# A streaming encoder step: key projections as one chunk of split products beside the first glu chunk

## The reference, cut

```python
h = rmsnorm(x, g_norm_mix[l]) * (1 + scale_m) + shift_m      # mod = silu(c) @ w_ada[l] + b_ada[l], six parts
q, k, v, iq, ik, iw, glu, sc, gates = split(h @ w_in[l])     # k, v, ik: 64 columns each
# A: indexer scores from iq, ik, iw choose keys; softmax attention over the chosen ones
# B: u = a * sigmoid(g); 31-tap depthwise convolution, layernorm, silu
# C: gated convolution of 3 taps
merged = g_a * (attn @ w_branch[0]) + g_b * (conf @ w_branch[1]) + g_c * (short @ w_branch[2])
x = x + gate_m * (merged @ w_out[l])
h = rmsnorm(x, g_norm_ffn[l]) * (1 + scale_f) + shift_f
x = x + gate_f * (swiglu(h) if l % 2 == 0 else top2_of_8_experts(h))
# outputs: final rmsnorm of x, new k, v, ik rows and the last convolution inputs of each layer
```

## Time and profile before

| | us |
|---|---|
| median of 3 runs | 1413.51 (1412.73 to 1415.42) |
| profiled execution | 1415.98 |
| its span | 1414.2 |
| PE busy | 1367.7 (97%) |
| DVE busy | 1012.7 (72%) |
| ACT busy | 783.3 (55%) |

### The profile page before, as it was taken

The page is one execution under the profiler, slowest core; times in us unless marked ns, Lnnn a source line. Parts: engine busy times, 40 slices in busy tenths (PEclk is TensorE's granted clock), DMA queues, the critical chain, the costliest instruction groups (busy, mean ns, idle before and its releaser), DMA issues.

```text
span 1414.2 us, 25016 instructions
## 1 busy us (share of the span) xinstructions
PE 1367.7 (97%) x9589; PEld 1211.1 (86%) x9589; DVE 1012.7 (72%) x1404; ACT 783.3 (55%) x1076; POOL 44.1 (3%) x66
## 2 busy tenths in 40 slices
PE   5999999999999999999999999998999999999997
PEld 4889999877899999997999998777588888888885
DVE  1477999875554444245789998755798988898887
ACT  1534447734453333235544486344778887788764
POOL 0010100000000000000001000000200000000030
PEclk9899999999999999999999999999999999999999
DMA  9957744224646867636578762245999999999993
GB/s 324 239 167 227 248 134 138 63 88 157 207 132 198 256 198 231 217 120 186 153 229 273 213 188 90 75 161 180 264 354 383 383 382 384 377 386 386 374 380 142
DMA packets 282693, 328.43 MB, mean 232 GB/s; under 512 B 34654, under 2 KB 192806, under 8 KB 282598
## 3 DMA queue, kind: packets, MB, share of 16 engines
q1 hardware_dynamic: 276146, 317.18, 68.4%
q0 software_dynamic: 1472, 5.24, 1.4%
q10 hardware_dynamic: 4980, 4.69, 1.0%
HBM read 312.41 MB, written 14.66 MB: 231 GB/s over the span
## 4 chain that ended last, share of the span: by engine, by line
PE 88%; DVE 6%; ACT 2%; issue 1%; DMA 1%; ACTq 0%; DVEq 0%; SPq 0%
PE mmp L915 15%; PE mmp L917 14%; PE mmp L916 14%; PE mmp L1413 8%; PE mmp L1414 8%; PE mmp L1415 8%; PE mmp L909 6%; DVE conv L2152 2%; PE px L980 1%; PE lg L980 1%; PE px L1181 1%; DMA ring<-in_w_ada_dram 1%; DMA wide<-in_w_dw_conf_dram 1%; PE lg L1137 1%; PE lg L1162 1%
## 5 line engine op out<-in xcount | busy, mean ns | idle before, releaser
L915 PE MATMUL mmp<-hT_hi,wm_hi 128*128 128x320 f32 (+1 forms) x976 | 311.3, 319 | 3.3 <-issue 3.1
L917 PE MATMUL mmp<-hT_hi,ring_lo 128*128 128x320 f32 (+1 forms) x976 | 303.0, 310 | 0.0
L916 PE MATMUL mmp<-hT_lo,wm_hi 128*128 128x320 f32 (+1 forms) x848 | 262.2, 309 | 0.0
L2063 DVE TENSOR_TENSOR ring_lo<-ring,wm_hi 128x1024 fp32r<-128x1024 f32 (+1 forms) x124 | 148.3, 1201 | 66.8 <-ACT wm_hi L1627 64.3
L915 PEld LDWEIGHTS mmp<-hT_hi,wm_hi 128*128 128x128 f32 (+1 forms) x976 | 183.6, 188 | 7.7 <-issue 5.5
L917 PEld LDWEIGHTS mmp<-hT_hi,ring_lo 128*128 128x128 f32 (+1 forms) x976 | 183.9, 188 | 0.2
L1627 ACT CAST wm_hi<-ring 128x1024 fp32r<-128x1024 f32 (+1 forms) x124 | 126.8, 1031 | 80.8 <-PE mmp L917 76.6
L916 PEld LDWEIGHTS mmp<-hT_lo,wm_hi 128*128 128x128 f32 (+1 forms) x848 | 160.0, 189 | 0.2
L1584 ACT ACTIVATE tmp<-mmp 128x320 f32<-128x320 f32 x68 | 29.8, 438 | 201.8 <-PE mmp L917 150.7
L2295 DVE TENSOR_TENSOR more_lo<-more,we_hi_a 128x2048 fp32r<-128x2048 f32 (+2 forms) x64 | 128.1, 2021 | 16.3 <-ACT we_hi_a L1811 16.2
L2152 DVE SCALAR_TENSOR_TENSOR conv<-u_conf,dwc,conv 128x350 f32<-128x350 f32 x240 | 132.6, 583 | 3.1
(11 more groups left out here) (408 smaller groups left out, 2848.6 us busy)
## 6 DMA issues: line engine op xcount, KB each, us to landing
ring<-in_w_in_dram SPq DMA_DIRECT2D x104, 512.0 KB, 4.9
ring<-in_w_exp_in_dram SPq DMA_DIRECT2D x64, 512.0 KB, 7.9
more<-in_w_exp_in_dram SPq DMA_DIRECT2D x64, 512.0 KB, 11.3
ring<-in_w_ada_dram SPq DMA_DIRECT2D x52, 512.0 KB, 6.9
more<-in_w_exp_out_dram SPq DMA_DIRECT2D x48, 512.0 KB, 6.4
wide<-in_w_ada_dram SPq DMA_DIRECT2D x44, 512.0 KB, 7.3
ring<-in_w_ffn_in_dram SPq DMA_DIRECT2D x44, 512.0 KB, 5.3
ring<-in_w_branch_dram SPq DMA_DIRECT2D x48, 256.0 KB, 2.9
```

Source lines behind the costliest of these rows:

```text
L915: nc.tensor.matmul(out, w_hi, x_hi, start=is_first, stop=False)
L916: nc.tensor.matmul(out, w_hi, x_lo, start=False, stop=False)
L917: return nc.tensor.matmul(out, w_lo, x_hi, start=False, stop=is_last)
L2063: V.tensor_tensor(mix_rows(ring_lo, l, s, r), mix_rows(ring, l, s, r), mix_hi(l, s, r).bitcast(F32), ALU.subtract).then_inc(mix_lo_ready, 1)
```

## The change

K and index-K become one split chunk `kik` of 64 + 64 columns, loaded once, the new chunk 0 of `SPLIT`; all the tables move up by one. Chunk 0 and glu 0 are worked together in a new PE function `first_chunks`: for each block f of h the three key products, and three blocks behind (`LEAD = 3`) the six glu products. DVE makes `hT_lo` two blocks behind the norm multiplication, ACT casts each block right after its scale. In layer 0 the casts and subtractions of the glu 0 weights are put between those blocks; in layer 1 those of both chunks are moved to the end of the layer-0 feed-forward, on DVE ahead of the last additions to x. The copies of the keys to both partition halves are made by ACT from PSUM (four large copies, then four small ones). In layer 0 the fifth modulation pair (m = 4) goes behind chunk 6 (glu 2), each later one takes the place of its follower, and pair 9 goes behind chunk 17, with its bank freed by the state copies. In layer 1 pair 7 stands behind `first_chunks`, and its turn one chunk later.

```diff
-ADA_AT_QKV = ((4,), (6, 7))
-ADA_AT_SPLIT = ({5: 5, 7: 6, 9: 7, 11: 8, 13: 9}, {7: 8, 9: 9, 11: 10, 13: 11})
+ADA_AT_QKV = ((), (6, 7))
+ADA_AT_SPLIT = ({6: 4, 8: 5, 10: 6, 12: 7, 14: 8, 17: 9}, {8: 8, 10: 9, 12: 10, 14: 11})
-SPLIT = ([("glu", 0), ("glu", 1), ("qkv", 2), ...
+SPLIT = ([("kik", 0), ("glu", 0), ("glu", 1), ("qkv", 2), ...
+LEAD = 3
...
# SP
+                    if s == 2:
+                        for m in ADA_AT_QKV[l][1:]:
+                            sp.wait_ge(chunk_done, ring_no["ffn", l - 1, NFFN - 1] + 1)
+                            ada_loads(l, m)
+                    if stage == "kik":
+                        v = slot_view(n % SLOTS, DC, P)
+                        load(n, [(v[:, :, r * HD:(r + 1) * HD], win[:, :, c:c + HD]) for r, c in enumerate((K0, IK0))])
...
# PE
+            def first_chunks(l):
...
+                def step(s, f):
+                    r, i = f // 4, f % 4
+                    q = pair_no[(SPLIT[s][0], l, SPLIT[s][1])]
+                    if f == 0:
+                        pair_wait(q)
+                    if i == 0:
+                        pe.wait_ge(mix_lo_ready, 2 * (NSPLIT * l + s) + r + 1)
+                    hi, lo = rows(s, r)
+                    for b in range(s + 1):
+                        c = slice(b * P, b * P + P)
+                        ins = three(mmp[:, 2 * (q % 2) + b, 0:T], hi[:, i, c], lo[:, i, c], hT_hi[:, f, :],
+                                    hT_lo[:, f, :], f == 0, f == DC - 1)
+                    if i == 3:
+                        ins.then_inc((half_done, chunk_done)[r], 1)
+
+                for f in range(DC + LEAD):
+                    if f < DC:
+                        pe.wait_ge(hT_lo_ready, DC * l + f + 1)
+                        step(0, f)
+                    if f >= LEAD:
+                        step(1, f - LEAD)
...
# ada_wait
+                    if m == ADA_AT_SPLIT[0][S_STATE + 1]:
+                        pe.wait_ge(st_copied, 3)
...
# ACT
+                    for r in range(2):
+                        mix_high(0, r)
...
                 for c in range(DC):
+                    norm_scale(2 * l, gain_of(0), shift_of(0), (c,))
                     act.wait_ge(h_ready, DC * 2 * l + c + 1)
                     copy(hT_hi[:, c, :], hT[:, c, :]).then_inc(hT_hi_ready, 1)
+                    if l == 0 and c in (1, 3):
+                        mix_high(1, c // 2)
                 if l == 0:
                     row_loads(1)
...
+                    if stage == "kik":
+                        for r, dst in enumerate((kT, ikT)):
+                            src = pair("kik", l, 0, 0)[r * HD:(r + 1) * HD, :]
+                            copy(dst[0:HD, 0:T], src)
+                            ins = copy(dst[HD:P, 0:T], src)
+                        ins.then_inc(pair_evac, 1)
+                        act.wait_ge(pair_evac, pair_no["kik", l, 0] + 1)
+                        for dst, dst_s in ((kT, kTs), (ikT, ikTs)):
+                            copy(dst[:, T:TW], dst[:, TP:T])
+                            ins = copy(dst_s[:, l, PAST:NKS], dst[:, TP:T])
+                        ins.then_inc(keys_copied, 1)
+                        return
...
# ACT, behind the loop of the layer-0 feed-forward
+                    for s in range(2):
+                        for r in range(2):
+                            mix_high(s, r, l + 1)
...
# DVE
+                norm_apply(2 * l, behind=hT_low, lag=2,
+                           beside={2: key_lows, 4: lambda: mix_low(1, 0), 6: lambda: mix_low(1, 1)} if l == 0 else ())
...
# DVE, in the loop of the layer-0 feed-forward
+                        if k == NFFN - 2:
+                            for s in range(2):
+                                for r in range(2):
+                                    mix_low(s, r, l + 1)
```

More of the change, by code:

```diff
@@ L136, in plan @@
     for l in range(DEPTH):
-        m = ADA_AT_QKV[l][0]
-        ring["ada", l, 2 * m], n = n, n + 1
-        if l:
-            ring["ada", l, 2 * m + 1], n = n, n + 1
-        for j in range(2):
-            chunk("qkv", l, j)
-        if l == 0:
-            ring["ada", l, 2 * m + 1], n = n, n + 1
+        for m in ADA_AT_QKV[l][:1]:
+            ada(l, m)
         for m in ADA_AT_QKV[l][1:]:
@@ L451, in build @@
         kv_copied = sem("kv_copied")
+        keys_copied = sem("keys_copied")
         sc_done = sem("sc_done")
@@ L705, in _ @@
                             clear_rows(j)
-                    if s == 3 and l == 0:
+                    if s == 4 and l == 0:
                         cache_loads()
@@ L1107, in _ @@
                     norm_sums(2 * l)
-                ada_half(l, ADA_AT_QKV[l][0], 0, (lambda: norm_spread(2 * l)) if l else None)
-                if l:
-                    ada_half(l, ADA_AT_QKV[l][0], 1)
-                pair_chunk("qkv", l, 0, h_rhs, blocks=((0, P),), width=P, each=h_each(2 * l))
-                pair_chunk("qkv", l, 1, h_rhs, blocks=((0, P),), width=P)
-                if l == 0:
-                    ada_half(l, ADA_AT_QKV[l][0], 1)
+                for m in ADA_AT_QKV[l][:1]:
+                    ada_half(l, m, 0, lambda: norm_spread(2 * l))
+                    ada_half(l, m, 1)
+                first_chunks(l)
                 for m in ADA_AT_QKV[l][1:]:
@@ L1218, in unit_tick @@
                         transposes(t - 1)
-                for s in range(NPROJ):
+                for s in range(2, NPROJ):
                     heads, ticks = HEADS_AT.get(s, ()), TICKS_AT.get(s, ())
@@ L1594, in shift_of, with mix_high @@
                     return lambda c: mods[:, l, 24 * which + c, 0:1]
+                def mix_high(s, r, l=l):
+                    n = ring_no[(SPLIT[s][0], l, SPLIT[s][1])]
+                    act.wait_ge(w_full[n % SLOTS], 32 * (n // SLOTS + 1))
+                    if s >= 2 and r == 0:
+                        act.wait_ge(half_done, NSPLIT * l + s - 1)
+                    if s >= 2 and r == 1:
+                        act.wait_ge(chunk_done, ring_no[(SPLIT[s - 2][0], l, SPLIT[s - 2][1])] + 1)
+                    copy(mix_hi(l, s, r), mix_rows(ring, l, s, r)).then_inc(mix_hi_ready, 1)
                 if l == 0:
@@ L1757, in _ @@
                         ada_evac(l, ADA_AT_SPLIT[l][s])
-                    if s == 0:
+                    if s == 1:
+                        for m in ADA_AT_QKV[l]:
+                            ada_evac(l, m)
+                    if s == 2:
                         for m in ADA_AT_QKV[l]:
@@ L2022, in norm_stats, with norm_apply @@
                 dve.wait_ge(rstd_spread, k + 1)
-            def norm_apply(k, behind=None, lag=0):
+            def norm_apply(k, behind=None, lag=0, beside=()):
                 for c in range(DC + 1):
+                    if c in beside:
+                        beside[c]()
                     if c < DC:
```

90 lines of the change are left out of this document (29 added, 61 removed).

## The result

The changed kernel takes 1416.72 us (median of 20 runs), the kernel before 1413.64 us beside it (20 runs): a ratio of 1.0019, 95% interval 1.0012 to 1.0026. Measured once more it took 1416.75 against 1413.89, 1.0021 (1.0012 to 1.0031). So the change makes the kernel slower, by 2.7 to 3.1 us; 1416.3 was predicted. By the count of its products it saves TensorE 5 us of work in each layer, and all of that is gone again, and a little more.

The account below looks back on a forecast made before the run. TensorE, 88% of the chain, was taken as the bound. Layer 0 (-1.0 + 1.5 + 2.0 = +2.5) and layer 1 (+3.0 - 4.0 + 1.3 = +0.3) give +2.8 on the 1413.5 median: 1416.3 us, range 1411.5 to 1419.0.

Parts of the forecast that it names:

- Layer 0, the front: Layer 0's key and glu 0 blocks: last scale ends at 49.0 us, PE through at about 55 (53 to 57).
- Layer 0, what is late next: Layer 0: loads on ACT's queue hold glu 1 until 58.5 us instead of 59.5; gain -1.0 (-0.6 to -4.5).
- glu 1 before 56: Layer 0: sign that the prediction is wrong, if glu 1 starts before 56 us; forecast start 58.5.
- The clock in layer 0: Layer 0, behind the pause ahead of glu 1: about 12 products at half clock, +1.5 us; 0 if it stays up.
- The sixth pair among the chunks: Layer 0's later chunks: six modulation pairs instead of five, with no idle PE time to hide it, +2.0 us (1.9 to 2.1).
- The wait for three copies: Layer 0: last modulation pair, behind the state transposes, waits for its bank; 0, at most one copy, 0.5 us.
- The end of the feed-forward: Before layer 1's norm: glu weights land at 640.4, subtractions delay the last addition to 647.0 us; +3.0 (+2.2 to +3.5).
- Layer 1, the keys: Layer 1's first chunks: -4.0 us, with the feed-forward's 3.0 -1.0; half clock on 11 products +1.3; layer +0.3.
- (b): One or both stretches stay at full clock: 1414.8 with layer 0, 1415.0 with layer 1, 1413.5 both; chance 0.27.
- (c): Layer 0 blocks overlap, queue drains faster, glu 1 starts before 56; with a faster layer 1, 1409.2 us; chance 0.12.
- (d): Layer 0: key weights land later than 35.4, their casts delay the first scale; +1.8, 1418.1 us, to 1420; chance 0.16.
- The base: Whole kernel: profiled execution before, 1415.98 us, lies 2.5 above the median 1413.5; same difference taken off the forecast.

Follow-up runs that it names:

- fillers: Changed kernel plus products nobody reads in PE's pauses ahead of layer 0's glu 1 and in layer 1's first block waits: 1414.22 us, ratio 1.0004.
- before_rows_sp: Kernel before, with the 13 small loads issued by SP behind its load of glu 1 instead of by ACT: 1414.20 us, ratio 1.0006.
- a_rows_on_sp: Changed kernel with the 13 small loads issued by SP behind the fourth chunk's load instead of by ACT: 1413.22 us, ratio 0.9989.
- e_pair4_cache: Changed kernel with layer 0's modulation pair 4 inside the cache transposes, five pairs left among the chunks: 1412.04 us, ratio 0.9988.
- b_tail: Changed kernel with layer 1's glu 0 casts and subtractions moved from the feed-forward's end into the norm and blocks: 1413.33 us, ratio 0.9994.
- b2_tail: Changed kernel with layer 1's glu 0 subtractions moved behind the last addition and behind the reciprocal, norm gains computed earlier: 1414.61 us, ratio 1.0007.
- c_pair4_gap: Changed kernel with layer 0's modulation pair 4 in the pause ahead of glu 1, five pairs left among the chunks: 1413.60 us, ratio 0.9995.
- best: Changed kernel with loads on SP, feed-forward's end rearranged, layer 1's pair 7 in block waits, layer 0's pair 4 in cache transposes: 1402.71 us, ratio 0.9925.

## Why the prediction held, step by step

The forecast of 1416.3 lies 0.4 us beside the 1416.72, and the mechanisms were the right ones, but that it is so close is partly luck. Glu 1 of layer 0 started 1.0 us earlier than I had put it, and the clock in layer 1 usually costs 1.3 us more; the two errors cancel.

**Layer 0, the front: right.** The last scale ended at 49.1 (49.0 predicted), the two chunks at 55.7 (55).

**Layer 0, what is late next: right in kind, 1 us too dear.** The queue of 13 loads holds glu 1, as the move to SP shows. It took 5.5 us and not 7.0, because the last entry took 0.54 us instead of the 2.06 of the earlier trace rows; glu 1 started 2.0 us earlier than before, not 1.0, and PE stood 1.80 us, not 3.5. What ends the wait is the last of the four key copies on ACT (57.41), the release of the PSUM pair, 0.36 us behind DVE's subtraction (57.05); I had the two ending together. I also misread the kernel before: the cast at 56.44 was qkv 2's, and glu 1 stood ahead of the loads. The sum doesn't suffer, as it goes from the start of glu 1, but two things exposed the wait and not one: the cover got shorter, and the list moved up by one, which put glu 1 behind the loads. My own sign of being wrong, glu 1 before 56, is a clock time and a bad sign: in the second profile glu 1 starts at 55.69, after the same pause (1.84 us), because all the blocks lie 2.0 us earlier.

**The clock in layer 0: right, with a wrong base.** 12 products at half clock, as predicted. Glu 1 to the first cache transposition takes 15.7 us with the fall and 14.1 to 14.3 without, so 1.5 us was the right size. It was there in four of the six profiles of the changed order with that pause idle, and in none with fillers, with pair 4 or without a pause. But the execution that I summed against had such a fall too, in glu 0, and before_rows_sp, the same kernel but for the 13 loads, has none behind the same pause. The fall is a draw in either kernel, so part of the +1.5 was in the base already.

**The sixth pair among the chunks: right.** +2.0 predicted, and 2.0 between the averages of the third stretch with six pairs and with five. The wait for three copies cost nothing that the timelines show.

**The end of the feed-forward: right.** Landing 640.4 predicted, 640.97 found; last addition 647.0 predicted, 647.23 found; +3.0 against the feed-forward's own end, and taking the two subtractions out brings 3.0 back.

**Layer 1, the keys: right in its sum by one profile, too cheap by the others.** The last stretch grew by 0.2 us in the first profile (+0.3 predicted), but by 1.5 in the second and in the two others whose edits lie elsewhere (a_rows_on_sp 27.35, e_pair4_cache 27.30). I had put 11 products at half clock; there were 11, 22, 22 and 22. For the usual case that term was mis-sized by 1.3 us (22 products instead of 11), and this is the distance from the predicted 0.3 to the 1.5 found, within 0.1.

**The rivals.** (b) happened in neither profile of the changed kernel; in layer 0 alone it did in b_tail and b2_tail, so it was a real case for single executions. With the fillers both stretches run at full clock, and their 1414.22 is within 1 us of its 1413.5. (c) needed glu 1 before 56; it is what a_rows_on_sp shows at 54.19, though its 1409.2 also needed a shorter tail. (d) did not come: the casts of the key weights ended at 35.33, ahead of the first scale; that began at 36.74 against 36.49, and this execution was 0.25 us later already at the last transposition ahead of it.

**The base.** I took the profiled execution of before (1415.98) as 2.5 us above the median. Against the profile of before_rows_sp it has 1.9 us more in the first stretch, mostly the fall in glu 0, and 1.45 in the second, a fall of 16 products instead of 10 behind the cache transposes; the third, with a shorter fall behind the feed-forward's norm (10 products instead of 18), gives 1.4 back. So the 2.5 are mostly draws of the clock and no property of the code, and taking the difference off was the right step.

## What to carry to other kernels

Work saved on the bounding engine is a gain only if what stood beside it finds another cover: here 13 DMA issues on ACT's queue, two subtractions on DVE and one modulation pair had cost PE little or nothing in their old places (at most the pauses of 1.98 and 1.11 us ahead of glu 0), and they came back as 1.8, 3.0 and 2.0 us. So before an edit shortens or reorders a stretch, list what else lies in it on the other queues and what then stands behind what, and move it first. And a pause of the matmul engine can cost twice, once itself and once in the half clock behind it (1.5 to 2.6 us here), so put real work into it rather than only shorten it.

## What the hardware showed that I had not expected

The fall of the clock behind a pause is not fixed by the program. Pauses of 1.80, 1.84, 1.85, 1.86 and 1.98 us ahead of a glu chunk were followed by 12 or 13 products at half clock, two of 1.99 by none, one of 1.41 by none. In layer 1 the same code had 11 or 22 of them, and in c_pair4_gap, which changes nothing there, one at most: the fall came some microseconds sooner (granted clock 0.76 from 641 to 651), and sums and modulation products bore it. So up to 1.5 us in layer 0 and 2.6 in layer 1 come and go from execution to execution, beside the start of the blocks, which moves by 2.7 us. The runs of one kernel spread over 3 to 8 us, but the five of best over 1.0.

The clock was up behind every wait of 1.4 to 2.4 us between dense stretches that modulation products of 128 columns by 32 rows filled (granted clock 1.00 behind the pause in layer 0, behind the cache transposes and in layer 1); the cache transposes show it best, three profiles against eleven. And once it was up it survived waits of 0.55 to 1.26 us between blocks with PE busy for 4.08 of 7.0 us, where without the fillers the same blocks ran at 0.50 with PE busy for 5.48 of 7.0. By the Trainium skill, TensorE: Matmul & The Clock Gate (What's actually happening), the throttled state is the default and activity lifts it; the traces agree, and these two windows show that the same blocks can run at either level, depending on what PE did ahead of them.
